# Gated recurrence of a float32 transformer stack: level matmuls on 32-column parts of the array, and the value units' eviction moved from VectorE to ScalarE

## What is computed

```python
def hgrn2_mixer(x, lb, w_in, g_norm, w_out):
    q, f, i, og = jnp.split(x @ w_in, 4, axis=-1)
    q = jax.nn.silu(q).astype(jnp.float32)
    log_f = jnp.logaddexp(jnp.log(lb), jnp.log1p(-lb) + jax.nn.log_sigmoid(f))
    k = (1.0 - lb) * jax.nn.sigmoid(-f)
    L = HG_CHUNK
    ...
    def step(S, inp):
        q_, k_, v_, g_ = inp
        b = jnp.cumsum(g_, axis=2)
        o_inter = jnp.einsum('bhtk,bhkv->bhtv', q_ * jnp.exp(b), S)
        diff = b[:, :, :, None, :] - b[:, :, None, :, :]
        decay = jnp.exp(jnp.where(causal[:, :, None], diff, -jnp.inf))
        A = jnp.einsum('bhtk,bhsk,bhtsk->bhts', q_, k_, decay)
        o_intra = jnp.einsum('bhts,bhsv->bhtv', A, v_)
        ...
    _, o = lax.scan(step, S0, (qc, kc, vc, gc))
    o = rmsnorm(from_chunks(o), g_norm)
    o = o.reshape(B, T, D_MODEL).astype(x.dtype) * jax.nn.silu(og)
    return o @ w_out
```

## Time and profile before

| | |
|---|---|
| median of 3 runs | 2605.75 us (2601.54 to 2607.52) |
| the profiled execution: its own time | 2607.22 us |
| its span, first to last instruction | 2605.4 us |
| PE busy | 2541.2 us (98%) |
| DVE busy | 1722.0 us (66%) |
| ACT busy | 1196.7 us (46%) |
| granted TensorE clock, mean | 0.991 |

### The profile page before, as it was taken

How to read it: one execution, slowest core, us unless ns; L and a number is a source line. 1 busy time by engine, 2 the same in 40 slices (tenths; PEclk the granted TensorE clock), 3 DMA queues, 4 the chain that set the end, 5 groups by cost and what they waited for, 6 DMA issues and landing times.

```text
span 2605.4 us, 50251 instructions
## 1 busy us (share of the span) xinstructions
PE 2541.2 (98%) x21448; PEld 2497.3 (96%) x21448; DVE 1722.0 (66%) x2221; ACT 1196.7 (46%) x1273; POOL 29.4 (1%) x62
## 2 busy tenths in 40 slices
PE   8999999999999999999988999999999999999998
PEld 8999999999998999999977999999999999999998
DVE  6557676586565765675576656755776657788765
ACT  5435354454344543454464444533535444544643
POOL 0000000000000000000000000000000000011000
PEclk9999999999999999999988999999999999999999
DMA  7554245545543455445532454554434554445352
GB/s 277 186 182 175 101 150 195 184 171 194 178 170 137 150 191 180 178 178 185 184 134 70 178 189 168 186 185 177 176 116 151 198 189 163 171 130 169 145 187 81
DMA packets 62676, 437.12 MB, mean 168 GB/s; under 512 B 7536, under 2 KB 8688, under 8 KB 10544
## 3 DMA queue, kind: packets, MB, share of 16 engines
q1 hardware_dynamic: 59984, 426.95, 45.6%
q0 software_dynamic: 2528, 7.74, 1.0%
HBM read 430.47 MB, written 1.05 MB: 166 GB/s over the span
## 4 chain that ended last, share of the span: by engine, by line
PE 83%; DVE 11%; ACT 4%; issue 2%; DMA 0%; SPq 0%; DVEq 0%; ACTq 0%
PE ps L679 54%; PE ps L713 19%; PE ps L697 5%; DVE w_lo L1588 3%; ACT w_hi L1170 2%; DVE scratch L1647 1%; DVE x L1706 1%; PE ps L834 1%; DVE right_lo L1641 1%; PE ps L958 1%; DVE right_hi L1638 1%; DVE left_lo L1641 1%; PE ps L981 1%; PE ps L967 0%; DVE left_hi L1638 0%
## 5 line engine op out<-in xcount | busy, mean ns | idle before, releaser
L1588 DVE TENSOR_TENSOR w_lo<-raw,w_hi 128x2048 fp32r<-128x2048 f32 x404 | 925.2, 2291 | 486.1 <-ACT w_hi L1170 485.9
L1170 ACT CAST w_hi<-raw 128x2048 fp32r<-128x2048 f32 x404 | 766.0, 1897 | 502.2 <-PE ps L713 249.1
L679 PE MATMUL ps<-right_hi,w_hi 128*128 128x256 f32 x2544 | 726.9, 286 | 7.2 <-DVE right_lo L1641 3.2
L679 PE MATMUL ps<-right_hi,w_lo 128*128 128x256 f32 x2544 | 720.3, 283 | 0.0
L679 PE MATMUL ps<-right_lo,w_hi 128*128 128x256 f32 x2544 | 720.2, 283 | 0.0
L679 PE MATMUL ps<-left_hi,w_hi 128*128 128x256 f32 x1968 | 563.8, 286 | 14.7 <-DVE left_lo L1641 11.9
L679 PE MATMUL ps<-left_hi,w_lo 128*128 128x256 f32 x1968 | 558.7, 284 | 0.0
L679 PE MATMUL ps<-left_lo,w_hi 128*128 128x256 f32 x1968 | 558.6, 284 | 0.0
L679 PEld LDWEIGHTS ps<-right_hi,w_hi 128*128 128x128 f32 x2544 | 488.5, 192 | 13.5 <-issue 5.0
L679 PEld LDWEIGHTS ps<-right_hi,w_lo 128*128 128x128 f32 x2544 | 488.7, 192 | 0.4
L679 PEld LDWEIGHTS ps<-right_lo,w_hi 128*128 128x128 f32 x2544 | 488.6, 192 | 0.0
(11 more groups left out here) (297 smaller groups left out, 3082.9 us busy)
## 6 DMA issues: line engine op xcount, KB each, us to landing
raw<-weights_dram SPq DMA_DIRECT2D x404, 1024.0 KB, 4.8
scratch<-scratch POOLq DMA_DIRECT2D x48, 64.0 KB, 1.9
raw<-weights_dram SPq DMA_DIRECT2D x2, 512.0 KB, 5.4
x<-x_t_dram SPq DMA_DIRECT2D x2, 512.0 KB, 6.9
scratch<-c_second_dram POOLq DMA_DIRECT2D x1, 1024.0 KB, 10.2
scratch<-p_t_dram POOLq DMA_DIRECT2D x4, 256.0 KB, 2.9
scratch<-mem_t_dram POOLq DMA_DIRECT2D x1, 1024.0 KB, 8.4
out_dram<-scratch SPq DMA_DIRECT2D x4, 256.0 KB, 2.5
```

Of the source, the lines that this page charges most:

```text
L679: last = nc.tensor.matmul(bank(e, ring)[:, half * T:(half + 1) * T], l, r, start=(k == 0 and j == 0 and half == 0), stop=(k == KC - 1 and ...
L1170: nc.scalar.copy(w_hi[:, m % SPLIT, :], raw[:, m % RAW, :]).then_inc(weights_hi, 1)
L1588: V.tensor_tensor(w_lo[:, m % SPLIT, :], raw[:, m % RAW, :], w_hi[:, m % SPLIT, :].bitcast(F32), ALU.subtract).then_inc(weights_split, 1)
```

## The change

Two parts, both inside `hg`.

The first: a level of w up to 16 is computed in parts of 32 tokens rather than 64, so 64 matmuls of 32 keys by 16 queries, whose results go to four 32-partition quarters in turn. Levels 5 and 6 (w = 32 and 64) keep their shapes.

The second: the values of units 8 to 11 are evicted from PSUM by ACT (an activation with function Copy and the token's scale) instead of by DVE, each behind ACT's cast for three units on. DVE gets one more wait, for these evictions, ahead of the eviction of unit 12.

```diff
+QUARTER = 32
...
-                            queries = P if w == HD else HD
-                            for t in range(P // queries):
-                                own_half = slice(at_ + t * HD, at_ + t * HD + queries)
-                                c = g * HD + t * queries // 2
-                                o = ps[t * HD:(t + 1) * HD, level_bank(l) + half, c:c + queries // 2]
+                            part = max(QUARTER, 2 * w)
+                            keys = min(part, HD)
+                            for t in range(0, P, part):
+                                c = g * HD + t // 2
+                                o = ps[t:t + keys, level_bank(l) + half, c:c + part // 2]
                                 last = nc.tensor.matmul(o.rearrange("p (n w) -> p n w", w=w),
-                                                        HG_SUFFIX[:, own_half.start:own_half.start + HD],
-                                                        upper(HG_PQ[:, own_half], w), start=True, stop=True)
+                                                        HG_SUFFIX[:, at_ + t:at_ + t + keys],
+                                                        upper(HG_PQ[:, at_ + t:at_ + t + part], w), start=True, stop=True)
...
+                def tokens(u):
+                    act.wait_ge(bank_read, e0 + u + 4)
+                    act.wait_ge(weights_used, n0 + u + 1)
+                    for b in range(TB):
+                        ins = nc.scalar.activation(HG_V[:, b, 256 * (u - 8):256 * (u - 7)], ps[:, (e0 + u) % 2, b * T:(b + 1) * T],
+                                                   ACT.Copy, scale=rcol[:, b:b + 1])
+                    ins.then_inc(bank_read, 1)
                 for u in range(8, 12):
                     high(n0 + u + SPLIT)
+                    tokens(u)
...
-                def tokens(u):
-                    scale_tokens(n0 + u, e0 + u, HG_V[:, :, 256 * (u - 8):256 * (u - 7)], 0, ring=2)
-
...
                 queries(3)
-                tokens(8)
                 low(n0 + 8 + SPLIT)
                 grow(0)
                 take_diagonal()
                 take(0)
-                tokens(9)
                 low(n0 + 9 + SPLIT)
...
-                tokens(10)
                 low(n0 + 10 + SPLIT)
...
-                tokens(11)
                 low(n0 + 11 + SPLIT)
                 grow(4)
                 grow(5)
+                dve.wait_ge(bank_read, e0 + 12 + 4)
                 gate(0)
```

## The result

The change made the kernel slightly slower: 2608.49 us median (2603.95 to 2609.65, 20 runs) beside 2602.36 (2600.98 to 2607.52, 20 runs), a ratio of 1.0015, 95% interval 1.0009 to 1.0021, or 3.9 us. (The medians alone lie 6.1 us apart; the text goes by the ratio.) The forecast was 2601.7 us and no change or a gain. The profiled execution took 2608.65 us, its span is 2606.9, and its mean granted clock 0.991, the same as before.

A forecast was written before the change was run, and what follows sets the result against it. PE, busy for 98% of the span, was taken to bound the kernel through its chain of waits. Levels 0, 2 and 3 pass on 0.82 + 0.43 + 0.82 = 2.07 us a recurrence, 4.1 for both: 2601.7 us, range 2598.5 to 2616.

The forecast's parts named there:

- The pace of the quarters: A changed level's burst on PE: four quarters side by side, 32 records of 31 ns each, 0.99 us; chance 0.48.
- The first rival: Level bursts on PE: only two tiles at a time, 1.98 us for 1.87, time 2606.4 us; chance 0.20.
- the third: Rival on level bursts: PE starts records no faster, 29 ns each, 3.7 us a burst, up to 2621.3 us; chance 0.24.
- the rule of the Trainium skill: Quarter records on PE: about 60 cycles overhead each, 25 ns, a burst 3.2 us, about 10 us slower in sum.
- What each level passes on: Gain reaching PE's chain of waits: levels 0 and 3 0.82 us each, level 2 0.43, levels 1 and 4 nothing.
- The sum of 2.07 us a recurrence: Levels 0, 2 and 3 on the chain: 0.82 + 0.43 + 0.82 us gained, 4.1 us for both recurrences.
- Part two: Evictions of units 8 to 11 on ACT: 0.9 us a unit, cost 0; alone gains 0 to 0.04 us a recurrence.
- it lets 0.8 us a recurrence through behind unit 11: Behind unit 11: with DVE's last eviction kept, DVE would end 0.8 us behind ACT's cast; already in the 2.07.
- The step that failed: Cost of a quarter level on PE: 0.99 us of loads plus 0.15 and 0.03 us, 1.17 us for 1.99.
- the listed cases: Four quarters side by side 0.48, two at a time 0.20, starts that bind 0.24; something else 0.08.
- what it gains becomes idle time ahead of level 2: nothing: Level 1, inside the detour through ACT and DVE: its gain passes on 0 us; idle time grows from 0.61 to about 1.4.

The follow-up runs named there:

- e1: Second part of the change alone against the kernel before: levels stay on halves, ACT evicts the values; 2603.51 us beside 2603.63, ratio 1.0000.
- e2: First part of the change alone against the kernel before: levels up to 16 on quarters, DVE still evicts; 2606.99 us, ratio 1.0014.
- r2: Changed kernel with levels 2 and 5 after 36 records of their units instead of 24, last cross-block product after 42 instead of 36; 2601.88 us, ratio 0.9994.
- f1: The shifted kernel: changed kernel with 64 more instructions (128 already met waits) at the start of TensorE's program; 2603.45 us beside 2603.8, ratio 1.000.
- r4: Changed kernel with quarters only in levels 0, 1 and 3, level 2 after 36 records, level 5 after 30, last cross-block product after 42; 2595.23 us, ratio 0.9965.
- c1: Control: the kernel before, in halves, with 64 more instructions at the start of TensorE's program; 2603.99 us beside 2604.37, ratio 1.000.
- r1: Kernel before with levels 2 and 5 after 30 records instead of 24, last cross-block product after 42 instead of 36; 2601.46 us beside 2603.8, ratio 0.9988.

## Why the prediction was wrong

- **The pace of the quarters** was right: 1.11 us for the starts of 128 records, 0.99 estimated from the loads. Four quarters work side by side. The first rival (two at a time, 1.98 us) and the third (starts that bind, 3.7 us) did not happen. Nor did the rule of the Trainium skill, TensorEngine Tiling (Array Packing), Instruction Overhead, by which a record would by the prediction's estimate have taken 25 ns; it took 8.7.
- **What each level passes on** was right where no stop covers it. Level 1's gain became idle time ahead of level 2 (0.77 us between starts), and in the shifted kernel level 4's became idle time ahead of level 5 (0.76). The sum of 2.07 us a recurrence was 1.9 in the shifted kernel's second one.
- **Part two** was right: 0.83 us a unit on ACT for 0.9, cost 0, and 0 alone (e1). That it lets 0.8 us a recurrence through behind unit 11 was not seen: with the quarters and without it (e2) the recurrences are even shorter (46.33 and 46.78 us) than with both (47.66 and 47.11), but stops and falls of the clock of different size cover the place, so this stays open.
- **The step that failed** is the one that I did not write: to the loads of a burst I added 0.15 us to the next unit's start and 0.03 us for its own, and charged nothing for issuing twice the instructions. I counted what the array does with a record, and not that 256 instructions in 1.11 us use up a 16 KB packet, of which no two start within 3.3 us of each other and which come behind a transfer of weights where one is running. In its place the runs showed PE halting until a packet had come, 2.97 and 2.62 us by starts in the two recurrences of the changed kernel. The stop of 2.97 us cost 1.7 net, since level 5 then had no wait left, and a fall of the clock followed it. I gave everything outside the listed cases 0.08.
- **The second step that failed**: "what it gains becomes idle time ahead of level 2: nothing". Idle time was priced at nothing. In the changed kernel the clock fell to 0.5 behind it in both recurrences, which cost 1.5 and 1.4 us.
- Behind longer stops it fell too. Each of the nine stops of 2.3 to 4.0 us in the kernels above has a stretch at 0.5 within it or behind it, and none of the stops up to 2.0 us does. The idle time of 1.4 us ahead of level 2 is less certain: right behind it the clock fell in 3 of the 10 recurrences that have it, and in none of the two where r2 fills it; f1 has as long an idle time ahead of level 5 in both recurrences, without a fall. So few cases do not show that the idle time causes the fall behind level 2; what decides is open.
- So the sign of the first recurrence's sum turned: -1.9 as forecast, +1.7 for the stop, +2.9 for two falls of the clock, +0.1 for the small stop, 2.8 of the 2.92 measured. The mechanism forecast took place, and two that were not forecast outweighed it.

## What to carry to other kernels

Cutting a matmul into smaller tiles multiplies instructions, and a burst of them can outrun their supply: count instructions for each microsecond beside the array's work, and look for idle time named "issue" in and behind the densest bursts, and for what the DMA engines do at that time. Before judging such a change, shift the program by a fraction of a packet; here 64 idle instructions took back what the change had cost. And a gain that lands as idle time of TensorE isn't yet a gain: move other work into it in the same edit, as r4 does, which took 9 us off where the change alone added 4.

## What the runs showed of the hardware

- A float32 matmul of 32 keys by 16 queries costs 8.7 ns a record when four column quarters alternate (128 records, starts over 1.11 us), a third of the densest pace of before.
- PE can halt for up to 4.0 us for its own instructions, by the compiled list 42 to 55 instructions short of a 16 KB packet's end: at 201 to 202 in the first recurrence and at 214 in the second, whichever kernel. It goes on 1.2 to 1.6 us behind the end of a packet. Packets start 3.34 us or more apart, and in the recurrences 185 of 191 start outside the transfers of weights or within 0.3 us of their end. The Trainium skill, Runtime: NRT & Kernel Launch, Instruction fetch mechanics, has the blocks of 16 KiB and 256 instructions, and says that crossing a boundary is mostly hidden, since instructions are dispatched more slowly than they are fetched. The runs agree for units and for levels in halves (no such idle time in the recurrences of before, e1, c1 and r1), and disagree for levels in quarters.
- 128 waits that are already met, folded into 64 instructions, fit into the 8.9 us of idle start; 128 instructions delayed it to 14.84 us, so such an instruction takes about 0.11 us (14.1 us from 0.7 us on, by 128). That is an estimate.
